# Activations rewritten by quarters at two stage entries, and dependent products one piece later, in a two-block transformer kernel

## What is computed

```python
# block one
u = rmsnorm(h, g_mix_pre); proj = u @ w_in
mix = (sigmoid(gla) * (dilated_attention(qa, ka, va) @ w_branch_a)
       + sigmoid(glb) * (stick_breaking(qb, kb, vb) @ w_branch_b)) @ w_out
h = h + rmsnorm(mix, g_mix_post)
up = causal_conv(rmsnorm(h, g_ffn_pre) @ w_up)
h = h + rmsnorm((gelu(gate_ff) * value) @ w_down, g_ffn_post)
h = h + sigmoid(h @ w_ple_gate) * (p @ w_ple_in)
# block two
proj = rmsnorm(x, attn_norm_g) @ w_in_2 + b_in_2      # q, k, v, u, two gates
attn = sliding_window_attention(q, k, v, sinks)       # 16 heads of 64
y = s5_ssm(u, ...)                                    # linear recurrence, 16 state tiles of 128
ssm = glu(gelu(y) @ w_glu)
x = x + (sigmoid(gate_attn) * (attn @ w_branch_attn) + sigmoid(gate_ssm) * (ssm @ w_branch_ssm)) @ w_out_2
val, gate = split(rmsnorm(x, ffn_norm_g) @ w_up_2)
x = x + (val * gelu(causal_conv(gate))) @ w_down_2
return rmsnorm(x, final_norm_g)
```

## Time and profile before

| | us |
|---|---|
| median of 3 runs | 2789.52 (2788.81 to 2790.98) |
| the profiled execution | 2789.55 |
| its span, first to last instruction | 2787.8 |
| TensorE busy | 2675.8 (96%) |
| VectorE busy | 1892.5 (68%) |
| ScalarE busy | 1362.4 (49%) |
| GpSimd busy | 300.7 (11%) |

### The profile page before, as it was taken

How to read it: one execution, slowest core, us unless ns; L and a number is a source line. 1 busy time by engine, 2 the same in 40 slices (tenths; PEclk the granted TensorE clock), 3 DMA queues, 4 the chain that set the end, 5 groups by cost and what they waited for, 6 DMA issues and landing times.

```text
span 2787.8 us, 46836 instructions
## 1 busy us (share of the span) xinstructions
PE 2675.8 (96%) x17118; PEld 2415.9 (87%) x17118; DVE 1892.5 (68%) x2476; ACT 1362.4 (49%) x1632; POOL 300.7 (11%) x325
## 2 busy tenths in 40 slices
PE   7999999997999999999988888999999999999998
PEld 6889999986888888888877888899888888888887
DVE  6555545757888888864476788867667777775444
ACT  5444454344555555444455344444455555554342
POOL 1000000023000000001100776700000000000000
PEclk9999999998999999999999999999999999999999
DMA  6665545563565555566555444455656556556664
GB/s 226 190 196 175 152 151 175 165 211 101 188 197 193 192 194 185 195 198 190 162 185 167 140 145 129 133 166 189 203 160 201 189 189 194 188 187 198 193 192 136
DMA packets 137640, 496.36 MB, mean 178 GB/s; under 512 B 15280, under 2 KB 15280, under 8 KB 137392
## 3 DMA queue, kind: packets, MB, share of 16 engines
q1 hardware_dynamic: 136800, 492.24, 56.2%
q10 hardware_dynamic: 720, 2.49, 0.2%
HBM read 492.57 MB, written 2.10 MB: 177 GB/s over the span
## 4 chain that ended last, share of the span: by engine, by line
PE 83%; DVE 8%; ACT 3%; DVEq 3%; issue 2%; DMA 1%; POOL 0%; ACTq 0%; POOLq 0%; SPq 0%
PE ps_w L419 82%; DVE w_lo L930 3%; ACT w_hi L634 1%; DVE act_w L961 1%; PE ps_o L419 1%; DVEq L1255 1%; PE ps_n L419 0%; DVE hT L984 0%; DVE rstd L945 0%; DVE proj L1306 0%; DVE scn L1250 0%; DVE pr L1256 0%; DVEq L1258 0%; DMA w_raw<-in_w_in 0%; DVEq L1214 0%
## 5 line engine op out<-in xcount | busy, mean ns | idle before, releaser
L930 DVE TENSOR_TENSOR w_lo<-w_raw,w_hi 128x1024 fp32r<-128x1024 f32 x928 | 1127.1, 1233 | 685.4 <-ACT w_hi L634 681.8
L634 ACT ACTIVATE w_hi<-w_raw 128x1024 fp32r<-128x1024 f32 x928 | 975.2, 1054 | 1044.2 <-PE ps_w L419 917.7
L419 PE MATMUL ps_w<-act_w,w_hi 128*128 128x512 f32 (+1 forms) x6912 | 1425.4, 353 | 47.0 <-DVE act_w L961 36.9
L419 PEld LDWEIGHTS ps_w<-act_w,w_hi 128*128 128x128 f32 x6912 | 1094.4, 190 | 183.9 <-issue 29.1
L419 PEld LDWEIGHTS ps_w<-act_w,w_lo 128*128 128x128 f32 x5600 | 736.6, 189 | 55.5 <-DVE w_lo L930 10.0
L419 PE MATMUL ps_w<-act_w,w_lo 128*128 128x256 f32 x5600 | 758.8, 278 | 7.2 <-DVE w_lo L930 7.1
L419 PE MATMUL ps_w<-f_w,w_hi 128*128 128x512 f32 x1408 | 351.5, 392 | 0.0
L419 PEld LDWEIGHTS ps_w<-f_w,w_hi 128*128 128x128 f32 x1408 | 251.3, 188 | 43.4
L419 PEld LDWEIGHTS ps_w<-f_w,w_lo 128*128 128x128 f32 x1408 | 186.8, 188 | 15.0
L1453 POOL COPY tab<-tab 128x512 f32<-128x512 f32 x6 | 3.9, 644 | 1815.1 <-ACT tab L645 1815.1
L419 PE MATMUL ps_w<-f_w,w_lo 128*128 128x256 f32 x1408 | 189.1, 277 | 0.0
(11 more groups left out here) (206 smaller groups left out, 1507.5 us busy)
## 6 DMA issues: line engine op xcount, KB each, us to landing
w_raw<-in_w_up SPq DMA_DIRECT2D x352, 512.0 KB, 4.6
w_raw<-in_w_in SPq DMA_DIRECT2D x252, 512.0 KB, 4.0
w_raw<-in_w_down SPq DMA_DIRECT2D x176, 512.0 KB, 4.1
w_raw<-in_w_out SPq DMA_DIRECT2D x64, 512.0 KB, 4.4
w_raw<-in_w_ple_gate SPq DMA_DIRECT2D x32, 512.0 KB, 4.4
w_raw<-in_w_branch_attn SPq DMA_DIRECT2D x16, 512.0 KB, 3.7
w_raw<-in_w_branch_a SPq DMA_DIRECT2D x8, 512.0 KB, 4.3
w_raw<-in_w_branch_b SPq DMA_DIRECT2D x8, 512.0 KB, 3.6
```

The source lines that it names most:

```text
L419: return pe.matmul(o, l, r, start=start, stop=stop, skip_group_check=True)
L634: act.activation(w_hi[:, k, 0:n, :], w_raw[:, k, 0:n, :], ACT.Copy).then_inc(hi_ready, 1)
L930: dve.tensor_tensor(w_lo[:, k, 0:n, :], w_raw[:, k, 0:n, :], w_hi[:, k, 0:n, :].bitcast(F32), ALU.subtract).then_inc(lo_ready, 1)
```

## The change

**Quarters.** `round_up` for in2 and up2 (n = 4, 5) waits for `piece_used` at the first piece of the stage minus 3 plus c, that is, for the last piece of the old stage that reads quarter c, instead of for the whole old stage. So that this comes early enough in the queues, the last pair of the gate stage moves on ScalarE and VectorE from ahead of in2 into the place beside its piece 2, and the last pair of out2 on VectorE from piece 0 of up2 to piece 2. `round_off` of quarter c stands beside piece c; before, quarter 0 stood ahead of the stage and c + 1 beside piece c.

**Products.** In mix the `tri` product goes from +3 to +4 and the output product from +5 to +6, with the VectorE and ScalarE steps between them; on TensorE the output product now stands ahead of the scores. In in2 the state tiles start at piece 8 in place of 11, the product with C goes from +5 to +6, the transposes of a head from +4 to +5, its output product from +6 to +7, and the copies behind them by one; ScalarE copies the turned scores of one head before it normalises the next. The turn tables go from pieces 8 and 9 to 4 and 5. The wait of the state tiles for the bias is now for as many pairs as they need.

```diff
-at_state = lambda n: 11 + 4 * n
+at_state = lambda n: 8 + 4 * n
...
-                for h in which(lambda h: at_stick(h) + 3, HEADS_B, n):
+                for h in which(lambda h: at_stick(h) + 4, HEADS_B, n):
                     pe.wait_ge(sp_ready, h + 1)
...
-                for h in which(lambda h: at_stick(h) + 5, HEADS_B, n):
+                for h in which(lambda h: at_stick(h) + 6, HEADS_B, n):
                     pe.wait_ge(w_ready, h + 1)
...
             def mixer_2(n):
...
-                    if m == 0:
-                        pe.wait_ge(biased_ready, 2)
+                    if m % 8 == 0:
+                        pe.wait_ge(biased_ready, m // 8 + 1)
...
-                for m in which(lambda m: at_state(m) + 5, STATE_TILES, n):
+                for m in which(lambda m: at_state(m) + 6, STATE_TILES, n):
...
-                for h in which(lambda h: at_head(h) + 4, HEADS_2, n):
+                for h in which(lambda h: at_head(h) + 5, HEADS_2, n):
                     pe.wait_ge(p_norm, 8 + h + 1)
...
-                for h in which(lambda h: at_head(h) + 6, HEADS_2, n):
+                for h in which(lambda h: at_head(h) + 7, HEADS_2, n):
...
                 act.wait_ge(*ready)
-                if n:
+                if n in (4, 5):
+                    act.wait_ge(piece_used, st.piece0 - 3 + c)
+                elif n:
                     act.wait_ge(piece_used, st.piece0)
...
-                for h in which(lambda h: at_stick(h) + LEAD + 4, HEADS_B, n):
+                for h in which(lambda h: at_stick(h) + LEAD + 5, HEADS_B, n):
                     act.wait_ge(lw_ready, h + 1)
...
-            def mixer_2(n):
+            def mixer_2(n, last_ple):
                 if n < 4:
                     round_up(4, n)
+                if n == 2:
+                    last_ple()
...
+                for h in which(lambda h: at_head(h) + LEAD + 6, HEADS_2, n):
+                    act.wait_ge(p_turned, 8 + h + 1)
+                    act.activation(pT2_buf, ps_t[1][:, 0:BLK], ACT.Copy).then_inc(pt_kept, 1)
                 for h in which(lambda h: at_head(h) + LEAD + 3, HEADS_2, n):
...
-                for h in which(lambda h: at_head(h) + LEAD + 5, HEADS_2, n):
-                    act.wait_ge(p_turned, 8 + h + 1)
-                    act.activation(pT2_buf, ps_t[1][:, 0:BLK], ACT.Copy).then_inc(pt_kept, 1)
-                for h in which(lambda h: at_head(h) + LEAD + 7, HEADS_2, n):
+                for h in which(lambda h: at_head(h) + LEAD + 8, HEADS_2, n):
...
-            ple_rest(3, 1)
-            ple_open(3, 1)
             act.wait_ge(halved, 1)
-            last = stream(st_in2, add_bias(st_in2), mixer_2)
+            def last_ple():
+                ple_rest(3, 1)
+                ple_open(3, 1)
+            last = stream(st_in2, add_bias(st_in2), lambda n: mixer_2(n, last_ple))
...
-                for h in which(lambda h: at_stick(h) + LEAD + 3, HEADS_B, n):
+                for h in which(lambda h: at_stick(h) + LEAD + 4, HEADS_B, n):
                     dve.wait_ge(cum_ready, h + 1)
...
-                if n == 0:
+                if n < 4:
+                    round_off(4, n)
+                if n == 2:
+                    ple_sum(3, 1)
                     ple_add(3, 1)
                     dve.drain()
-                round_off_beside(4)(n)
-                if n in (8, 9):
-                    turn_tables(n - 8)
+                if n == 7:
+                    root(4)
+                if n in (4, 5):
+                    turn_tables(n - 4)
...
-                for b in which(lambda b: at_state(STATE_BLOCK * b + 3) + LEAD + 4, 4, n):
+                for b in which(lambda b: at_state(STATE_BLOCK * b + 3) + LEAD + 6, 4, n):
                     dve.wait_ge(x_used, STATE_BLOCK * b + 4)
...
-            ple_sum(3, 1)
-            round_off(4, 0)
...
-            round_off(5, 0)
             def up_beside(piece):
-                if piece == 0:
+                if piece < 4:
+                    round_off(5, piece)
+                if piece == 2:
                     last_out()
                     dve.drain()
-                round_off_beside(5)(piece)
+                if piece == 7:
+                    root(5)
```

More of the change, by code:

```diff
@@ L524, in mixer_1 @@
                     turn_values(7)
-                for h in which(at_stick, HEADS_B, n):
-                    if h == 0:
-                        pe.wait_ge(sc_read, 8)
-                    q, k = proj1[:, QB + h, :], proj1[:, KB + h, :]
-                    mm(ps_a[0][:, 0:TOK], k[:, 0:P], q, True, True)
-                    mm(ps_a[0][:, TOK:BLK], k[:, P:TOK], q[:, P:TOK], False, True).then_inc(zb_ready, 1)
-                for h in which(lambda h: at_stick(h) + 3, HEADS_B, n):
-                    pe.wait_ge(sp_ready, h + 1)
-                    if h == 0:
-                        pe.wait_ge(v_kept, 8)
-                    mm(ps_t[0][:, 0:TOK], tri, sp_b[:, 0:TOK], True, False)
-                    mm(ps_t[0][:, P:TOK], ones, sp_b[:, TOK:BLK], False, True)
-                    mm(ps_t[0][:, TOK:BLK], tri, sp_b[:, TOK:BLK], False, True).then_inc(cum_ready, 1)
-                for h in which(lambda h: at_stick(h) + 5, HEADS_B, n):
+                for h in which(lambda h: at_stick(h) + 6, HEADS_B, n):
                     pe.wait_ge(w_ready, h + 1)
@@ L547, in mixer_1 @@
                     mm(ps_o[:, P:TOK], v[:, P:TOK], t_b[:, TOK:BLK], False, True).then_inc(ob_ready, 1)
+                for h in which(at_stick, HEADS_B, n):
+                    if h == 0:
+                        pe.wait_ge(sc_read, 8)
+                    q, k = proj1[:, QB + h, :], proj1[:, KB + h, :]
+                    mm(ps_a[0][:, 0:TOK], k[:, 0:P], q, True, True)
+                    mm(ps_a[0][:, TOK:BLK], k[:, P:TOK], q[:, P:TOK], False, True).then_inc(zb_ready, 1)
+                for h in which(lambda h: at_stick(h) + 4, HEADS_B, n):
+                    pe.wait_ge(sp_ready, h + 1)
+                    if h == 0:
+                        pe.wait_ge(v_kept, 8)
+                    mm(ps_t[0][:, 0:TOK], tri, sp_b[:, 0:TOK], True, False)
+                    mm(ps_t[0][:, P:TOK], ones, sp_b[:, TOK:BLK], False, True)
+                    mm(ps_t[0][:, TOK:BLK], tri, sp_b[:, TOK:BLK], False, True).then_inc(cum_ready, 1)
             def mixer_2(n):
```

## The result

The kernel after the change takes 2769.59 us (median of 4 runs, 2769.22 to 2769.73), the kernel before beside it 2789.86 us: a ratio of 0.9925, 95% interval 0.9912 to 0.9937. The predicted time was 2770.0 us. The profiled span fell from 2787.8 to 2768.0 us.

A forecast was written before the change was run, and what follows sets the result against it. VectorE, with its handshake with ScalarE, was taken to bound the middle of in2. Savings of 6.1 (mix) + 10.7 (in2) + 2.9 (up2) = 19.7 us took 2789.5 to 2769.8 us; range 2760 to 2780, some 0.8.

The forecast's parts named there:

- `mix`: Stage mix: all four TensorE waits for `sp_b` vanish with the products one piece later; 6.1 us, bounds 5 and 6.3.
- Entry to `in2`: Start of in2: pieces 0 to 2 run without waiting, piece 3 waits some 8.8 us; 2.7 us, bounds 0 and 9.2.
- Head start at piece 20: In in2, VectorE is 4.3 us ahead at piece 20, which contains the entry's 2.7.
- The middle: in2 from piece 20: 4.5 of 6.1 us of VectorE's other waits go, its instructions the same; bounds 0 and 6.1.
- Rival E: GpSimd's operations fall on VectorE's subtractions in in2: a `w_lo` rises by 0.4 us, total 2795.4 us; chance 0.05.
- The lag at piece 76: End of in2: last products come at piece 74, reducing TensorE's lag behind VectorE; 1.9 us, bounds 0 and 4.1.
- Entry to `up2`: Start of up2: a new 2.4 us wait at piece 1 replaces 5.3 us lost; 2.9 us, bounds 1.2 (slow clock) and 5.3.

The follow-up runs named there:

- mix_only: Kernel before with only the mix stage's edit: `tri` product at +4, output product at +6, ahead of the scores; 2783.35 us, ratio 0.9973.
- state_undone: Kernel after with in2's state tiles back on the old schedule (11 + 4n, products at +5); 2779.79 us, ratio 0.9962.
- light_pool: Kernel after with ScalarE's bias one piece later and, from the third state tile, GpSimd computing only a few columns; 2734.35 us, ratio 0.9797.
- heads_only: Kernel before with only in2's heads moved: transposes at +5, output product at +7, turned-scores copy ahead of the normalising; 2795.75 us, ratio 1.002.
- quarters_only: Kernel before with only the quarters: `round_up` released by each quarter's last reader, last pairs beside piece 2; 2786.66 us, ratio 0.998.
- heads_undone: Kernel after with in2's heads taken back: transposes at +4, output product at +6, turned-weights copy one piece earlier; 2773.27 us, ratio 0.9942.
- loads_later: Kernel after with SyncE issuing the first four broadcast loads of the state tiles at pieces 5 to 8 of in2, not 2 to 5; 2759.99 us, ratio 0.9887.
- bias_later: Kernel after with ScalarE's bias of each state column in in2 one piece later; 2742.46 us, ratio 0.9827.
- last-quarter edit: Kernel after with the last quarter's rewriting (`last_out`) beside piece 1 of up2 instead of piece 2; 2768.26 us, ratio 0.9919.

## Why the prediction came out right, step by step

**`mix`**, 6.1 us predicted, 7.2 in the trace and 7.0 by the medians of `mix_only`. The step was right and its upper bound of 6.3 too tight. It counted the waits with their named releaser (5.7 + 0.6); the idle time fell by 6.3, and the remaining 0.9 us is TensorE's busy time, 233.46 to 232.54 for the same 1975 matmuls.

**Entry to `in2`**, 2.7 us predicted, 3.1 measured (piece 3 began 3.08 us earlier after the end of `gate`; 1.6 of these TensorE lost again in the slow piece, 3.78 us against 2.15, but VectorE kept its lead: with the quarters alone it reaches piece 20 2.6 us earlier); the wait was forecast at 8.8 us and is 8.54, the slow piece is there. The chain through `ple_used` and SyncE's queue was played through in the right order: the `bc_pad` load came 7.1 us after the end of `gate`, predicted 6.7.

**Head start at piece 20**, 4.3 us predicted, 3.3 measured (1578.13 - 1504.01 against 1569.94 - 1499.13). The part that failed is the state tiles' own. The 4.3 held 2.7 from the entry and so 1.6 from them. VectorE reaches piece 20 71.1 us after the end of `gate` with the state tiles taken back (`state_undone`) and 71.5 with the quarters alone, against 70.8 in the change: they give 0.3 to 0.7 us, and by themselves they cost 1.2. Which instruction holds VectorE there was not traced. A new wait stands behind it that no step had: TensorE waits 3.8 us for `vpad` (L1214) at piece 22, where VectorE pads the keys in the same piece as a state step; VectorE being the pace, it shows in no end.

**The middle**, 4.5 us predicted with an upper bound of 6.1, 9.3 measured. This is the term that was mis-sized. The waits did what the step said: 5.4 us of other waits became 1.0, and 0.7 us for a state product became 0, 5.1 us together. The other 4.5 us is VectorE's busy time. The step read "from there VectorE's instructions are the same" and took their durations as given. They are a sum of the work and of what GpSimd adds: by `light_pool`, where a little of GpSimd's work is left, at most 170.9 us are VectorE's own, so at least 27.2 us are interference before, 22.8 after, and 33.5 with the bias moved.

**Rival E** named that interference and priced it in one direction. It is real, it changes with the alignment of the two engines, and it went the other way: the mean `w_lo` fell from 1377 to 1311 ns, where the rival wanted 1700. That it is the heads' move that takes most of it is measured (193.7 to 194.5 against 197.4 with the heads undone). That it comes from which instructions meet can be read one by one in the traces. The product L1257 of the kernel before, without and with an instruction of GpSimd already running:

```profile
1637.28 0.41 DVE L1257 TENSOR_TENSOR pr<-scn,rot 128x256 f32<-128x256 f32 x1
...
1758.05 0.93 POOL L1501 TENSOR_TENSOR tab<-scn,rot 128x256 f32<-128x256 f32 x1
...
1758.30 0.96 DVE L1257 TENSOR_TENSOR pr<-scn,rot 128x256 f32<-128x256 f32 x1
```

It takes 0.41 us in 5 of its 14 places and 0.95 to 0.97 in 9, and in each of the 9 a product or sum of GpSimd had begun less than 0.3 us before it. In the change it takes 0.42 in 6, 0.67 or 0.68 in 3 and 0.94 to 0.97 in 5; with the bias moved 0.96 to 0.99 in 12 of 14. A `w_lo` with no instruction of GpSimd beside it takes 1.22 us on average in all three; there are 7, 13 and 7 of these among the 56, and 25, 20 and 25 take over 1.3 us. Why the heads' move shifts the two engines against each other in this way was not followed.

**The lag at piece 76**, 1.9 us predicted, 0.5 measured: TensorE began piece 76 6.05 us after its `w_lo` was ready, 5.57 before, so it did not come closer to VectorE; what the end of `in2` gains over piece 76 comes from the last four pieces, 11.0 us from there to the end against 12.0, which no longer have products between them. With the heads moved and the state tiles not (`heads_only`, `state_undone`) the part from VectorE's piece 76 to the end takes 16.9 us against 18.8, the 1.9 of the forecast; with both moved it takes 18.3. So 4.3 + 4.5 + 1.9 = 10.7 us stand against 3.3 + 9.3 + 0.5 = 13.1.

**Entry to `up2`**, 2.9 us predicted, 1.65 measured. The wait for `hT` came where it was forecast, 1.94 us for 2.4; what was left out is that TensorE's clock fell behind it (mean granted clock 0.61 from 2026.10 to 2029.14), 3.25 us for eight products against 2.00, and 1.59 against 1.07 for the next eight: 1.8 us. The lower bound of 1.2 had it ("slow clock again"). It does not fall each time. Seven traces have this wait of 1.93 to 1.95 us; in four (the change, `quarters_only`, `heads_undone`, `loads_later`) the clock fell, in three it stayed at 1.00. Of `bias_later`:

```profile
2000.98 2.13 PE L419 MATMUL ps_w<-act_w,w_hi 128*128 128x512 f32 x8 [1.94 <-DVE hT L1359]
```

In these three `up2` is 3.2 us shorter than before, near the 2.9 of the forecast.

The total was right by errors of opposite sign: 3.5 us too little in `mix` and `in2`, against 1.3 too much in `up2` and 2.3 us that this execution lost in stages which the change does not touch (`in`, and those between `mix` and `gate`). The Trainium skill, page "TensorE: Matmul & The Clock Gate", section "HAM oscillation — how this bites in real kernels", says that idle stretches bring the half clock. Both slow pieces of the change agree, after 8.54 and 1.94 us of idle time, but how long the wait was does not decide it here: after 2.40 us in `loads_later` the piece ran in 2.15 us, and after the same 1.94 us in `bias_later` in 2.13. What else decides is open.

What stays open: why the heads alone lengthen VectorE's waits by 4 us where with the state tiles they add 1, beyond the collision at every twelfth piece, which both kernels have; why their median is 5.4 us longer where the trace shows 0.9 in `in2`; and what the last-quarter edit is worth in the median.

## What to carry to other kernels

When TensorE waits for engines that themselves wait, write down one engine's stretch as busy + waits + gaps and find the wait that repeats in every slot: a single operation that ScalarE does one place too early cost this kernel as much as the whole change gained, and on the kernel before, moving it alone gives the same time (2769.2 and 2769.6 us). A part of a schedule is not worth what it is worth alone: test it by taking it back from the finished change too. And hold no duration fixed on VectorE beside GpSimd, least of all when a wait is removed: in `bias_later` 26.6 us of waits went and VectorE's busy time rose by 10.7.

## What the runs showed of the hardware

VectorE's instructions with two inputs in SBUF are lengthened by GpSimd's by amounts that were larger than expected. In the stretch a product of 256 columns (L1257 before, L1276 in the others) takes 424 ns on average with most of GpSimd's work left out, 764 before the change and 911 with the bias moved; a scan 680, 742 and 964; a `w_lo` 1225, 1377 and 1336. With one input in PSUM a product of that size takes 412 to 425 ns in all of them, and a reduction of `s_buf` over 256 columns 409 or 410. One product goes from 0.41 to 0.96 us when it starts behind a product or sum of GpSimd. The Trainium skill, page "SBUF — State Buffer", section "Who interferes with whom", says that an instruction of VectorE with two SBUF inputs and one of GpSimd that reads SBUF contend, and calls the port pair that they share an exclusive lock; the rows agree. In `bias_later` at least 33.5 of 204.4 us of VectorE's busy time in the stretch are this (204.4 - 170.9), so an edit that removed 26.6 us of waits gave back 10.7 of them there.
